# Delta rule: gates and keys written to DRAM right behind the norms, outputs of 128 tokens in one product, the convolution's first tap on ScalarE

## What is computed

```python
proj = h @ dn_w_in                                  # q, k, v, gates, xq, z
qkv = silu(causal_depthwise_conv(qkv, conv_w))      # 4 taps along the tokens
q, k = l2_norm(q) * 128 ** -0.5, l2_norm(k)         # 12 heads of q and k, 24 of v
g = -exp(a_log) * softplus(a + dt_bias); beta = sigmoid(b)
# per head, in 4 chunks of 64 tokens: gc = cumsum(g)
decay = exp(gc[:, None] - gc[None, :])              # lower triangle
m = beta * (k @ k.T) * decay (strictly lower) + I
u0, w = solve(m, v * beta), solve(m, k * beta * exp(gc))
u = u0 - w @ state
o = (q * exp(gc)) @ state + ((q @ k.T) * decay) @ u
state = exp(gc[-1]) * state + (k * exp(gc[-1] - gc)).T @ u
x = x + (concat(rms_norm(o), xa) * silu(z)) @ w_out
```

## Time and profile before

| | |
|---|---|
| median of 3 runs | 3081.11 us (3077.78 to 3085.37) |
| profiled execution | 3085.42 us |
| its span, first to last instruction | 3083.6 us |
| mean granted TensorE clock | 0.966 |
| TensorE busy | 2882.2 us (93%) |
| DVE, ACT, POOL busy | 1926.8, 1388.1, 371.2 us |

### The profile page before, as it was taken

How to read it: one execution, slowest core, us unless ns; L and a number is a source line. 1 busy time by engine, 2 the same in 40 slices (tenths; PEclk the granted TensorE clock), 3 DMA queues, 4 the chain that set the end, 5 groups by cost and what they waited for, 6 DMA issues and landing times.

```text
span 3083.6 us, 46686 instructions
## 1 busy us (share of the span) xinstructions
PE 2882.2 (93%) x19490; PEld 2708.7 (88%) x19490; DVE 1926.8 (62%) x2849; ACT 1388.1 (45%) x2351; POOL 371.2 (12%) x338
## 2 busy tenths in 40 slices
PE   6999997869899999999998999998999999999896
PEld 6999997858888899899997999998888899988775
DVE  5456655833223454556445865776887788878786
ACT  5345434235555433444435313433555555555454
POOL 0000000011111100000500001222212211112320
PEclk9999998979999999999998999999999999999998
DMA  4443434423222355454443357999899988899893
GB/s 182 177 151 137 164 111 148 143 81 96 85 80 81 145 183 184 155 183 152 157 158 131 138 201 268 360 373 340 339 353 376 355 328 324 317 349 358 315 349 144
DMA packets 112050, 668.49 MB, mean 217 GB/s; under 512 B 28336, under 2 KB 28552, under 8 KB 33920
## 3 DMA queue, kind: packets, MB, share of 16 engines
q1 hardware_dynamic: 86976, 496.93, 44.3%
q0 software_dynamic: 23712, 164.11, 14.4%
q10 hardware_dynamic: 1152, 4.47, 0.4%
HBM read 651.54 MB, written 13.30 MB: 216 GB/s over the span
## 4 chain that ended last, share of the span: by engine, by line
PE 68%; DVE 12%; DMA 10%; ACT 7%; issue 2%; POOL 0%; SPq 0%; ACTq 0%; DVEq 0%
PE PS L999 68%; DMA raw<-in_pv 6%; DVE WL L1613 4%; DVE m L1604 3%; ACT WH L2290 3%; ACT m L2275 2%; DMA m<-in_pv,keep 1%; ACT L2275 1%; ACT m L2276 1%; DVE m L2115 1%; DMA raw<-in_w_kv 0%; PE PS L1002 0%; DVE m L1607 0%; DMA m<-s_kk 0%; DVE m L1800 0%
## 5 line engine op out<-in xcount | busy, mean ns | idle before, releaser
L1613 DVE TENSOR_TENSOR WL<-raw,WH 128x1024 fp32r<-128x1024 f32 x804 | 986.7, 1234 | 667.3 <-ACT WH L2290 666.0
L2290 ACT CAST WH<-raw 128x1024 fp32r<-128x1024 f32 x804 | 837.5, 1046 | 566.2 <-PE PS L999 386.0
L999 PE MATMUL PS<-m_4096r,WH 128*128 128x256 f32 x5184 | 1001.4, 294 | 46.7 <-DVE m L1604 16.4
L999 PEld LDWEIGHTS PS<-m_4096r,WH 128*128 128x128 f32 x5184 | 829.5, 196 | 70.8 <-DVE m L1604 18.4
L999 PE MATMUL PS<-m_4096r,WL 128*128 128x256 f32 x2592 | 745.0, 287 | 0.0
L999 PE MATMUL PS<-m_8192r,WH 128*128 128x256 f32 (+1 forms) x2560 | 562.9, 314 | 16.6 <-issue 11.1
L999 PE MATMUL PS<-WH,m_896r 128*128 128x512 f32 x1536 | 524.7, 394 | 27.3 <-DVE m_896r L2208 27.1
L999 PEld LDWEIGHTS PS<-m_4096r,WL 128*128 128x128 f32 x2592 | 508.9, 196 | 0.0
L999 PEld LDWEIGHTS PS<-m_8192r,WH 128*128 128x128 f32 x2560 | 399.8, 194 | 20.0 <-issue 11.7
L999 PE MATMUL PS<-m_8192r,WL 128*128 128x192 f32 (+1 forms) x1792 | 405.8, 273 | 0.0
L999 PE MATMUL PS<-WL,m_896r 128*128 128x512 f32 x1024 | 401.3, 392 | 0.0
(11 more groups left out here) (228 smaller groups left out, 1868.0 us busy)
## 6 DMA issues: line engine op xcount, KB each, us to landing
raw<-in_pu SPq DMA_DIRECT2D x128, 1024.0 KB, 6.9
raw<-in_pv SPq DMA_DIRECT2D x128, 1024.0 KB, 8.4
raw<-in_w_qkv SPq DMA_DIRECT2D x48, 1024.0 KB, 4.8
raw<-in_w_o SPq DMA_DIRECT2D x48, 1024.0 KB, 4.8
raw<-in_w SPq DMA_DIRECT2D x40, 1024.0 KB, 4.8
raw<-in_w_z SPq DMA_DIRECT2D x32, 1024.0 KB, 5.9
raw<-in_w_kv SPq DMA_DIRECT2D x16, 1024.0 KB, 4.8
raw<-in_w_q SPq DMA_DIRECT2D x16, 1024.0 KB, 4.8
```

The source lines that it names most:

```text
L999: return e.matmul(o, l, x, start=start, stop=stop)
L1613: tt(WL[:, k, :], raw[:, n % NRAW, h * 1024:h * 1024 + 1024], WH[:, k, :].bitcast(F), ALU.subtract).then_inc(S["lo"], 1)
L2290: e.copy(WH[:, k, :], raw[:, n % NRAW, h * 1024:h * 1024 + 1024]).then_inc(S["hi"], 1)
```

## The change

Five things change.

1. `iv_turn`, with the round trip of the gates through DRAM, stands right behind `rn_root`, ahead of the twelve scaling products; it now waits for the root, whose PSUM bank it uses. The scaling products do k first and q behind it.
2. The six products k @ k.T stand right behind the norms with one part between them (3.7 before). `iv_decay` waits for the gates alone; 20 parts stand between the third decay and the first `iv_scale`, which is what waits for k @ k.T. Each step of the substitution is followed by 4 parts (2 at both ends), and `iv_out` by 16. The inverse has 171 parts in all.
3. The buffers are laid out so that the six zero tiles no longer overlap what is being stored, and POOL writes them behind the loads of k @ k.T.
4. In `dn_o` the share of the outputs that comes from within 128 tokens is one product with all 128 rows of u, for chunks 0 and 1 behind the second u and for chunks 2 and 3 behind the fourth. The step `o0` is gone; the update `s0` stays.
5. The multiplication by the last tap of the convolution is an activation on ACT (Copy with a scale), which DVE's three additions wait for (`tap`).

```diff
@@ invert @@
-        self.do("iv_turn")
         for c in range(6):
-            yield
             self.do("iv_product", c)
+            yield 1
         self.do("iv_store")
-        for _ in range(4):
-            yield
         for b in range(3):
             self.do("iv_decay", b)
-            yield
+            yield 3
+        yield 20
         for b in range(3):
             self.do("iv_scale", b)
-            yield
+            yield 4
         for j in range(31):
             self.do("iv_step", j)
-            yield
+            yield 4 if 4 <= j < 27 else 2
         self.do("iv_out")
         for g in range(2):
             self.do("dn_load", g)
-        for _ in range(3):
-            yield
-        st["i"] = True
+        yield 16
@@ mix @@
-        inverse, credit = self.invert(st), 0.0
-        while not st["i"]:
-            next(fz)
-            credit += INV_RATE
-            if credit >= 1:
-                credit -= 1
-                next(inverse, None)
+        for parts in self.invert():
+            for _ in range(parts):
+                next(fz)
@@ TensorE: iv_turn, iv_product @@
                 p.wait_ge(*at("keep", 1))
-                p.wait_ge(*at("qkn", 12))
+                p.wait_ge(*at("rn_root", 1))
...
-                p.wait_ge(*at("qkn", 12))
-                if b == 2:
-                    p.wait_ge(*at("iv_gates", 1))
+                p.wait_ge(*at("qkn", 7 + c))
@@ TensorE: dn_o @@
+                def from_state(h):
+                    o = PS[:, bC, h * 256 + n * 64:h * 256 + n * 64 + 64]
+                    return mm(o, blk(dn_s(g), h), blk(dn(g, "qd"), 2 * h + t)[:, b:b + 64], False, False)
+
+                def from_within(h, start, stop):
+                    o = PS[:, bC, h * 256 + t * 128:h * 256 + t * 128 + 128]
+                    return mm(o, dn_u(g)[:, h * 128:h * 128 + 128], blk(dn(g, "dT"), 2 * h + t), start, stop)
+
                 for h in range(2):
-                    i = 2 * h + t
-                    o = PS[:, bC, h * 256 + n * 64:h * 256 + n * 64 + 64]
+                    if n == 1:
+                        from_within(h, h == 0, False)
                     if n:
-                        mm(o, blk(dn_s(g), h), blk(dn(g, "qd"), i)[:, b:b + 64], True, False)
-                    m = mm(o, dn_u(g)[b:b + 64, h * 128:h * 128 + 128],
-                           dn(g, "dT")[b:b + 64, i * 128 + b:i * 128 + b + 64], n == 0, True)
+                        m = from_state(h)
+                    if n == 3:
+                        m = from_within(h, False, h == 1)
@@ DVE: conv, iv_decay, iv_scale @@
-                v.wait_ge(*at("used", done(n)))
-                v.wait_ge(*at("n_lo", 32))
-                if k >= 2:
-                    v.wait_ge(*at("silu", k - 1))
-                v.step(one(tmp, PS[:, bank, 0:256], vc("conv", widx * 4 + 3), ALU.mult))
+                v.wait_ge(*at("tap", k + 1))
...
-                v.wait_ge(*at("ld_iv", 96))
+                v.wait_ge(*at("ld_gb", 64))
...
                 v.wait_ge(*at("iv_exp", b + 1))
+                v.wait_ge(*at("ld_kk", 32))
@@ ACT: silu @@
+                a.wait_ge(*at("used", done(n)))
+                a.wait_ge(*at("n_lo", 32))
+                act(CONV[k % 2], PS[:, bank, 0:256], ACT.Copy, scale=vc("conv", widx * 4 + 3)).then_inc(S["tap"], 1)
                 a.wait_ge(*at("conv", k + 1))
                 act(dst, CONV[k % 2], ACT.Silu).then_inc(S["silu"], 1)
@@ POOL: iv_store, iv_out @@
                         S["ld_iv"], 16)
+                for g in range(2):
+                    for name in ("T", "U", "BT"):
+                        e.tensor_copy(c4(dn(g, name)), bc(C("zero"), 4)).then_inc(S["iv_zero"], 1)
...
-                g_.wait_ge(*at("iv_stored", 96))
-                for g in range(2):
-                    for name in ("T", "U", "BT"):
-                        e.tensor_copy(c4(dn(g, name)), bc(C("zero"), 4)).then_inc(S["iv_zero"], 1)
```

More of the change, by code:

```diff
@@ L27 @@
 FILL = 1.0
-INV_RATE = 0.27
 POOL = (6, 7, 4, 5, 2, 3, 0, 1)
@@ L255, in qk_norm @@
         self.do("rn_root")
+        self.do("iv_turn")
         yield
         yield
-        for c in range(12):
-            self.do("rn_spread", c)
+        for n in range(12):
+            self.do("rn_spread", n)
             yield
@@ L339, in mix @@
     def mix(self):
-        st = {"v": 0, "n": False, "i": False, "g": 0, "z": set(), "y": set(), "p": set()}
+        st = {"v": 0, "n": False, "g": 0, "z": set(), "y": set(), "p": set()}
         fz = self.vz(st)
@@ L932, in ct_last, with crossed @@
             return CT[:, 448 * c + ND + 128:448 * c + 448]
+        def crossed(w):
+            w.wait_ge(*at("ca_value", 8))
+            w.wait_ge(*at("xa", 8))
+            w.wait_ge(*at("ca_exp", 8))
+            w.wait_ge(*at("ca_pt", 8))
         def sync_program(e):
@@ L1263, in rn_sum, with rn_spread @@
                     m.then_inc(S["rn_sum"], 1)
-            def rn_spread(c):
-                b = 2 + (c + 1) % 6
+            def rn_spread(n):
+                b, c = 2 + (n + 1) % 6, (n + 6) % 12
                 p.wait_ge(*at("rn", 1))
@@ L1270, in rn_spread @@
                 p.wait_ge(*at("ca_pt", 8))
-                if c >= 6:
-                    p.wait_ge(*at("qkn", c - 5))
+                if b == 2:
+                    p.wait_ge(*at("iv_gates", 1))
+                if n >= 6:
+                    p.wait_ge(*at("qkn", n - 5))
                 for i in range(4):
@@ L1727, in conv @@
                 tmp = CONV[k % 2]
-                v.wait_ge(*at("used", done(n)))
-                v.wait_ge(*at("n_lo", 32))
-                if k >= 2:
-                    v.wait_ge(*at("silu", k - 1))
-                v.step(one(tmp, PS[:, bank, 0:256], vc("conv", widx * 4 + 3), ALU.mult))
+                v.wait_ge(*at("tap", k + 1))
                 for s in (1, 2, 3):
-                    v.own()
+                    if s > 1:
+                        v.own()
                     t = stt(tmp[:, s:256], PS[:, bank, 0:256 - s], vc("conv", widx * 4 + 3 - s), tmp[:, s:256], ALU.mult,
@@ L2368, in ca_value, with silu @@
                     e.copy(tile(XA, 2 * h + i), PS[:, 6 + i, 0:256]).then_inc(S["xa"], 1)
-            def silu(k, dst):
+            def silu(k, dst, widx, bank, n):
+                a.wait_ge(*at("used", done(n)))
+                a.wait_ge(*at("n_lo", 32))
+                act(CONV[k % 2], PS[:, bank, 0:256], ACT.Copy, scale=vc("conv", widx * 4 + 3)).then_inc(S["tap"], 1)
                 a.wait_ge(*at("conv", k + 1))
@@ L2375, in qk_out @@
                 a.wait_ge(*at("used", done(KV + 15)))
-                silu(i, tile(QT if i % 2 else KT, i // 2))
-            def crossed(w):
-                w.wait_ge(*at("ca_value", 8))
-                w.wait_ge(*at("xa", 8))
-                w.wait_ge(*at("ca_exp", 8))
-                w.wait_ge(*at("ca_pt", 8))
+                silu(i, tile(QT if i % 2 else KT, i // 2), i // 2 if i % 2 else 12 + i // 2, i % 2, QK_ + i)
             def v_out(n, i):
                 crossed(a)
-                silu(v_index(i), tile(VT, i))
+                silu(v_index(i), tile(VT, i), 24 + i, n % 2, VZ + n)
             def z_out(n, i):
@@ L2754, in iv_out @@
                     rows = slice(48 * h, 48 * h + 48)
-                    for name, x in (("iu", f(88, 2048)), ("it", f(96, 2048)), ("im", IV_E[:, 2048:3072])):
+                    for name, x in (("iu", IV_U), ("it", IV_T), ("im", IV_E[:, 2048:3072])):
                         e.dma_start(by_chunk(scratch[name], h), x[rows, :]).then_inc(S["iv_stored"], 16)
-                g_.wait_ge(*at("iv_stored", 96))
-                for g in range(2):
-                    for name in ("T", "U", "BT"):
-                        e.tensor_copy(c4(dn(g, name)), bc(C("zero"), 4)).then_inc(S["iv_zero"], 1)
             def dn_y(g):
```

34 lines of the change are left out of this document (20 added, 14 removed).

## The result

The changed kernel takes 3027.5 us (median of 4 runs, 3025.9 to 3029.4), the kernel before 3079.5 us beside it (4 runs, 3071.2 to 3085.4): ratio 0.983, 95% interval 0.981 to 0.986. It is faster by 52 us; the forecast was 3036 us in a range of 3020 to 3060 us. The profiled execution took 3026.0 us with a span of 3024.1 us.

The account below looks back on a forecast made before the run. The prediction took TensorE's work, plus stretches where it stands still, to bound the kernel. From the profiled 3085.4 us, 30 and 18 us off gave 3037 us (3033 us from the median); it took 3036 us, range 3020 to 3060 us.

Parts of the forecast that it names:

- Term 1, the inverse: Way to group 0: starts 43.3 us earlier, less 13.0 us of leftover filler; gain 30 us, bounds 15 and 37 us.
- the turned gates: Ahead of the scaling products: TensorE now waits for the root, losing some 2 us, bounds 1 to 4 us.
- the stall at the decays: Near 460 us: ScalarE's decay work delays a cast and its split, a new TensorE stall of 6 us.
- the first scaling: In the inverse: VectorE reaches it at about 476.3 us, without waiting for k @ k.T, back at 470.2 us.
- the 18 parts left over: Filler still to be done behind the last group: 18 x 0.72 = 13.0 us, taken off the inverse's gain.
- the 26 us worked out from it: The inverse's gain by estimate if three table switches, each with the skill's drain, ended the inverse 4 us later.
- Term 2, the outputs: Output steps in 12 groups: 1.9 us less each, 23 us, cut to 1.5 us each; 18 us, bounds 5 and 23.
- Term 3, the tap elsewhere: Units of q, k and remaining values: 0 us, covered by TensorE's lead; otherwise 5 us in either direction.
- The groups did get faster: Rival on the groups: they don't get faster, saved matmuls become waits, outputs give 0 to 5 us; 3049 us, chance 0.14.
- The wait did move in part: Rival at the decays: the stall grows through ScalarE's queue, the inverse gains only 15 us; about 3052 us, chance 0.10.
- The slower case: Rival in the 48 convolution units: the tap waits in ScalarE's queue and delays TensorE; 3105 us at 1.5 us each, chance 0.03.
- The time from group 0 to the filler's end: Sign in the group stage: about 405 us, with 13 us more filler and 18 us less of outputs.

Follow-up runs that it names:

- e6: The kernel before with only the outputs within 128 tokens joined into one product; 3049.6 us.
- e3: The kernel before with the tap on ScalarE and the joined outputs, its inverse untouched; 3047.1 us.
- e1: The changed kernel with the outputs of a group computed per chunk as before; 3046.8 us.
- e8: The changed kernel with 20 more parts of filler behind the inverse, loads of groups 0 and 1 issued behind the 16th; 3014.4 us.
- e7: The changed kernel with the three decays 10 parts of filler apart and one part more in all; 3037.1 us.
- e9: The changed kernel with 20 more parts of filler behind the inverse, loads of groups 0 and 1 issued behind the 35th; 3009.3 us.
- e4: The changed kernel with GpSimd's six copies of zeros behind the landing of the inverse's stores, as before; 3031.4 us.

## Why the prediction was right, and where it wasn't

The sum was right, 48 us forecast against 51.7 us in the stage. From the kernel before over e6 (the outputs) and e3 (the tap) to the changed kernel (the inverse) the two stretches shorten by 26.8, 6.0 and 18.9 us, which together is the 51.7 us. But two terms of the sum were off in opposite directions, by 6 us and by 7 to 12 us, so that it came out this near is in part luck.

**Term 1, the inverse: 30 us forecast, 24 us measured.** Its way to group 0 was nearly right: 41.6 us shorter against the root, where I had 43.3 us against the span's start. Step by step: the turned gates cost about 1 us and not 2 (the first scaling product came 7.4 us after the root, 6.5 us before); the stall at the decays was 6.3 us, 6 forecast; the first scaling began at 472.3 us (476.3 forecast), as much earlier as the root was; DVE's stretch to the end of `iv_out` was 102.6 us (101.2 forecast); group 0 started 19.8 us behind it (19.7 forecast), with TensorE idle 14.8 us. The step that failed is the price of the 18 parts left over: I took 0.72 us each, the rate of the dense filler; e3 shows 17.5 us for them, not 13.0 us. That is 4.5 of the 6 us, and the later start against the root is the other 1.7 us. Within this term the tap has 6 us (4.5 us forecast). The exp behind a table load again started 1.29 us after it (454.05 and 455.34 us), as in the earlier trace rows. The Trainium skill's drain of 1.38 us behind each load (ScalarE: Activation LUTs, What ACT_TABLE_LOAD costs) isn't in this trace either; that the term came out below the 26 us worked out from it has the other cause above.

**Term 2, the outputs: 18 us forecast, 25 to 30 us measured.** My own count from the steps was 23 us, and the rows behind it hold (0.65, 1.74, 1.19 and 1.06 us where I had 0.6, 1.6, 1.2 and 1.1 us). I had cut it to 1.5 us a group because I thought that part of the saving would become waits. Hardly any of it did: in e6 the waits for the reciprocal are 16.3 us and those for the copies of u 12.1 us, against 15.2 and 11.4 us, and all idle time together grew by 2.3 us. What I left out was the clock, 0.94 in the earlier trace rows, which was 0.96 with this edit, and with it the filler's own matmuls, 4.7 us less. The upper bound of 23 us was too low.

**Term 3, the tap elsewhere: 0 us forecast, 0.5 to 3.0 us measured** behind group 0, inside the bound of 5 us and no more than that stretch's scatter of 3.3 us; what it does ahead of the root is open.

**The rivals.** The groups did get faster (e6). The wait did move in part, to the decays, but by no more than forecast: term 1's lower bound of 15 us is 9 us away. The slower case has no trace: the tap takes time off in all three pairs. The time from group 0 to the filler's end was forecast as 405 us and is 394.8 us; the sum of my own terms would have been 404.9 + 13.0 - 18 = 400 us, so this line of the prediction wasn't even consistent with its terms.

## What to carry to other kernels

Price work that is moved by the rate of the stretch it moves to (0.87 to 1.08 us a part here among the groups, 1.26 us by e1's profile), not by its best rate where it leaves. Where whole runs scatter by 9 us in a stage that nobody touched, cut the trace at marks of the program, and profile a kernel twice: one pair of profiles then agreed within 0.2 us in both stretches, another within 0.1 us in one and 3.3 us in the other. And a load that waits on a queue belongs as late in that queue as its user allows: where the loads ahead of group 0 stood early, ScalarE waited 12.4 us for weights (e8) and 19.8 us (e7); with the loads 19 parts of filler later (e9) the 12.4 us of e8 fell to 0.8 us, and the two stretches were 4.1 us shorter.

## What the runs showed of the hardware

- Two two-input instructions of VectorE took 3.18 us beside GpSimd's copies and 2.35 us without them (e4); the six copies took 5.86 us there and 3.38 us late, when VectorE was idle and no load of k @ k.T was under way.
- With the joined outputs the granted clock among the groups was 0.95 or 0.96 (0.94 in e7, whose TensorE stood 7.6 us longer there), without them 0.93 or 0.94, in both orders of the inverse.
- Two matmuls of the filler took 0.79 us right behind a stall of 6.3 us and 0.40 us at full clock.
